# The three light experts of a streamed expert stage move from passes 2, 3 and 8 to passes 4, 6 and 8

## The chip, the cores and the metric

The kernel runs on one core of one Trainium2 chip. The metric is the device time of one execution in microseconds (us). Beside the runs that were only timed there is one profiled execution, and all rows below come from it.

## The reference, cut to what matters

An encoder trunk of two layers over 16 meta tokens and 256 frames, model width 1024. Each layer has a mixer (retention beside latent attention) and then a feed-forward part: a dense SwiGLU of width 3584 in the first layer, and eight SwiGLU experts of that width, of which each token takes two, in the second. A final RMS norm follows, and the meta tokens are dropped. The change touches only the order in which the expert part goes through its experts:

```python
def moe_swiglu(h, router_w, w_gate, w_up, w_down):
    logits = (h @ router_w).astype(jnp.float32)
    top_val, top_idx = lax.top_k(logits, TOP_K)
    gates = jax.nn.softmax(top_val, axis=-1)
    ...
    out = jnp.zeros_like(h)
    for e in range(N_EXPERTS):
        out = out + gate_dense[..., e:e + 1] * swiglu(h, w_gate[e], w_up[e], w_down[e])
    return out
```

## The kernel before, in words

Up to about 521 us the kernel runs the first layer, the mixer of the second, and the routing. Then come the experts, in eight **passes**. Everything is float32, and every expert's weights are streamed from HBM once: 24 **units** of 1792 KB, loaded two at a time as 12 **pairs** of 3584 KB (`load_two`, line 469, whose DMA is on line 473; single units, `load_one`, line 463, whose DMA is on line 466, at the very start and in the last half of the last expert).

**The ring.** The weights land in twelve slots, six pairs. SyncE (SP) issues the load of pair j only when TensorE has used up pair j - 6: it waits for `w_used` to reach `... + 2 * j + 2 - MOE_SLOTS` (line 471). TensorE adds to `w_used` as it finishes each unit. So the pair that TensorE works on and the five after it are all that can have landed or be on their way. All these loads go through one queue, in order.

**The passes.** For each expert, tokens are gathered into three tiles of 32 columns (capacity 96). For three **light** experts two tiles do (capacity 64), and TensorE leaves out tile 0: `tiles=LIGHT if it in LIGHT_AT` on line 1138, and `LIGHT` for the last pass on line 1143. A pass does `up` for four groups of columns (16 units) and then `down` (8 units). A light pass thus reads the same 44 MB of weights as a full one and does two thirds of the matmuls. The passes 0 to 5 are written out, the passes from 6 up to the last stand in a loop (line 1141), and the last one is always light. This text counts passes from 0 as the code does, so the last one is pass 7.

**Which expert stands where.** Expert 0 is always first, since its weights are loaded before the routing is known. The others are ranked by their number of tokens on VectorE (`ordering`, lines 1779 to 1808). The result, `at_pass`, gives each expert its pass: before, the lightest of the seven goes last (pass 7), the next two go to passes 1 and 2, and the rest follow by size. `order_sb` is the inverse table, which SP reads to know whose weights to load next (`ordered`, line 500); `order_ready` tells that it is there. GpSimd (POOL) uses `at_pass` to build the gather table (line 580).

**Around the passes.** ScalarE (ACT) applies the SiLU (L1385) and scales what leaves a pass (L1395), VectorE (DVE) multiplies and transposes (L1824, L1827), POOL gathers the tokens of a later pass (L625) and adds the results of the pass before into HBM (L634). ACT, DVE and POOL treat all passes alike, with three tiles. Each pass of ACT begins with the small copy on L1375.

Of the kernel before, what the change touches and what calls it, by code (L numbers as in the profile page):

```python
# [37 lines left out]
ALU = mybir.AluOpType  # L38
# [16 lines left out]
EXPERTS = 8  # L55
# [3 lines left out]
SMALL = CAP - TOK  # L59
LIGHT = range(TILES_OF - SMALL // TOK, TILES_OF)  # L60
LIGHTS = 3
LIGHT_AT = [EXPERTS - 1, *range(1, LIGHTS)]
BIG = 1e30
LATE_AT = 10240
GAIN_AT = 14000
# [114 lines left out]
def build(nc, stream, experts, h0, gains, router_w, fnorm, consts, out):  # L180
    with ExitStack() as ctx:
# [54 lines left out]
        at = [0]  # L236
# [112 lines left out]
        def col(c, n=P):  # L349
            return c_sb[:, c:c + n]  # L350
# [314 lines left out]
        def _(pe):  # L665
# [471 lines left out]
            for it in range(EXPERTS - 2):  # L1137
                expert(it, tiles=LIGHT if it in LIGHT_AT else range(TILES_OF), first=it == 0)
            pe.wait_ge(rounds_ready, 1)
# [319 lines left out]
        def _(dve):  # L1459
            V = nc.vector  # L1460
            chain = [0]

            def link(ins, inc=None):

                if inc is not None:
                    ins.then_inc(inc, 1)
                    dve.wait_ge(inc, 1)
                    return
                chain[0] += 1
                ins.then_inc(link_sem, 1)  # L1470
                dve.wait_ge(link_sem, chain[0])
# [266 lines left out]
            def routing():  # L1738
# [36 lines left out]
                link(V.reciprocal(v12[:, :, 3:4], v12[:, :, 3:4]))  # L1775
                V.tensor_tensor(v12[:, :, 2:3], v12[:, :, 2:3], v12[:, :, 3:4], ALU.mult).then_inc(gates_in, 1)
                ordering()

            def ordering():

                E = EXPERTS
                number, total = col(C_IOTA, E), bank[3][:, 0:E]
                size_rank, light, at = least[:, :], key[:, :], at_pass[:, :]
                by_size = cmp_a[:, 0:E, 0:E - 1]
                at_place = cmp_b[:, 0:E, :]
                dve.wait_ge(total_done, 1)
                link(V.scalar_tensor_tensor(out=key[:, :], in0=total, scalar=float(E), in1=number, op0=ALU.mult, op1=ALU.add))
                link(V.memset(key[:, 0:1], BIG))

                link(V.tensor_tensor(by_size, key[:, 1:E].unsqueeze(1).to_broadcast([P, E, E - 1]),  # L1790
                                     key[:, :].unsqueeze(2).to_broadcast([P, E, E - 1]), ALU.is_lt))
                link(V.tensor_reduce(size_rank, by_size, axis=AX.X, op=ALU.add))
                V.tensor_scalar(light, size_rank, float(LIGHTS), float(CAP - SMALL), ALU.is_lt, ALU.mult)
                link(V.tensor_scalar(at, size_rank, 0.0, E - 1.0, ALU.is_equal, ALU.mult))
                V.tensor_tensor(v_total, light, total, ALU.add)
                link(V.tensor_tensor(at, at, size_rank, ALU.add))
                link(V.memset(at[:, 0:1], 0.0))
                V.tensor_reduce(cnt[:, 0:1], v_total, axis=AX.X, op=ALU.max)
                link(V.tensor_tensor(at_place, at.unsqueeze(1).to_broadcast([P, E, E]),
                                     number.unsqueeze(2).to_broadcast([P, E, E]), ALU.is_equal))  # L1800
                V.tensor_scalar(cnt[:, 1:2], cnt[:, 0:1], float(CAP), float(PASSES - EXPERTS), ALU.is_gt, ALU.mult)
                V.tensor_scalar(cnt[:, 2:3], cnt[:, 0:1], float(CAP), float(ROUNDS - 1), ALU.is_gt, ALU.mult)
                link(V.tensor_tensor(at_place, at_place, number.unsqueeze(1).to_broadcast([P, E, E]), ALU.mult))
                V.tensor_scalar(rounds_sb[:, 1:2], cnt[:, 1:2], EXPERTS - 1.0, None, ALU.add)
                V.tensor_scalar(rounds_sb[:, 0:1], cnt[:, 2:3], 1.0, None, ALU.add).then_inc(rounds_ready, 1)
                link(V.tensor_reduce(v_total, at_place, axis=AX.X, op=ALU.add))
                V.scalar_tensor_tensor(out=at, in0=light, scalar=float(SLOT_COLS), in1=at, op0=ALU.mult, op1=ALU.add)
                link(V.tensor_copy(order_sb[:, :, 0], v_total), order_ready)
# [76 lines left out]
            for t in range(2):  # L1885
                if t:
# [7 lines left out]
                                       op0=ALU.mult, op1=ALU.mult).then_inc(res_ready, 1)  # L1894
# [115 lines left out]
```

## Time and profile before

| | us |
|---|---|
| median of 3 runs (lowest to highest) | 1352.09 (1351.71 to 1352.82) |
| profiled execution, its own time | 1352.45 |
| span of that execution, first to last instruction | 1350.6 |
| TensorE busy in the span | 1294.5 |
| expert passes, from about 521 us to the end of the last matmuls at about 1341 us | 820 |
| granted TensorE clock, mean | 0.988 |

The span is the part that the rows show; the profiled execution's own time has 1.85 us around it. Times in the trace are counted from the span's start. "PE" is TensorE's matmuls and "PEld" its weight loads, SPq is SyncE as it issues DMAs. A DMA's time to landing runs from its issue by SP until its semaphore tells that all of it is there, so it holds the time that it stood in the queue.

### The profile page before, as it was taken

The numbers are of one execution on the slowest core, as the hardware profiler recorded it, in microseconds if no ns is written. First come the engines' busy times: TensorE is split into PE (matmuls) and PEld (weight loads), VectorE is DVE, ScalarE is ACT, GpSimd is POOL, SyncE is SP. The second block draws the span as 40 slices with busy tenths as digits, with TensorE's granted clock in tenths as the row PEclk, the third lists the DMA queues.
The fourth block names the chain that finished last, engine by engine and source line by source line (L and its number), as shares of the span: only waits on it lengthen the run. The fifth ranks groups of instructions, "written<-read, shape, count | busy, mean of one in ns | idle before, by whom it ended". The sixth has DMA issues, their size and how long they took to land.

```text
span 1350.6 us, 31070 instructions
## 1 busy us (share of the span) xinstructions
PE 1294.5 (96%) x14058; PEld 887.0 (66%) x14058; DVE 469.0 (35%) x821; ACT 341.3 (25%) x593; POOL 83.4 (6%) x113
## 2 busy tenths in 40 slices
PE   9999999999999999999987889999999999999886
PEld 8889999999998996456452254465465456446333
DVE  7767866777687663110201000100100110110121
ACT  8666543334367643000100000000000000000011
POOL 0000000000000004201010001001001001001000
PEclk9999999999999999999999889999999999999999
DMA  9316555544442589999999999999999999999994
GB/s 371 112 63 242 200 183 187 188 165 179 170 150 72 185 321 424 417 417 412 422 429 419 432 427 419 432 428 416 431 427 421 429 427 426 421 429 425 414 425 189
DMA packets 34783, 443.89 MB, mean 329 GB/s; under 512 B 5664, under 2 KB 7840, under 8 KB 12256
## 3 DMA queue, kind: packets, MB, share of 16 engines
q1 hardware_dynamic: 28944, 434.14, 77.8%
q0 software_dynamic: 5424, 7.51, 2.0%
q8 instruction: 110, 1.80, 0.5%
q10 hardware_dynamic: 288, 0.29, 0.1%
q14 instruction: 17, 0.14, 0.0%
HBM read 438.20 MB, written 5.93 MB: 329 GB/s over the span
## 4 chain that ended last, share of the span: by engine, by line
PE 79%; DMA 16%; DVE 2%; ACT 2%; issue 1%; SPq 0%; ACTq 0%; DVEq 0%
PE bank L677 78%; DMA moe_pair<-experts 15%; DVE w_pairs L1476 1%; DMA ring<-stream 1%; PE bank L681 0%; PE bank L775 0%; DVE nmx L1561 0%; ACT scratch L1233 0%; PE bank L781 0%; ACT w_pairs L1155 0%; ACT scratch L1232 0%; ACT scratch L1230 0%; DVE parts L1490 0%; PE bank L1122 0%; DVE sq L1554 0%
## 5 line engine op out<-in xcount | busy, mean ns | idle before, releaser
L677 PE MATMUL bank<-moe_pair,hT 128*32 128x448 f32 x5376 | 517.1, 546 | 23.6 <-DMA moe_pair<-experts 22.8
L677 PE MATMUL bank<-parts,w_pairs 128*128 128x272 f32 (+1 forms) x3360 | 427.4, 289 | 1.5 <-DVE parts L1490 0.9
L677 PEld LDWEIGHTS bank<-parts,w_pairs 128*128 128x128 f32 x3360 | 421.8, 188 | 5.4 <-issue 2.7
L677 PEld LDWEIGHTS bank<-moe_pair,hT 128*32 128x32 f32 x5376 | 206.6, 111 | 330.1 <-issue 298.2
L1824 DVE SCALAR_TENSOR_TENSOR hT<-bank,slot_norm,scratch 128x224 f32<-128x224 f32 x96 | 40.6, 423 | 694.9 <-ACT scratch L1385 694.9
L677 PE MATMUL bank<-moe_pair,scratch 128*32 128x256 f32 x4704 | 263.5, 384 | 16.1 <-DMA moe_pair<-experts 16.1
L677 PEld LDWEIGHTS bank<-moe_pair,scratch 128*32 128x32 f32 x4704 | 184.3, 111 | 96.6 <-issue 25.0
L1476 DVE TENSOR_TENSOR w_pairs<-ring,w_pairs 128x2048 fp32r<-128x2048 f32 x68 | 154.7, 2290 | 32.2 <-ACT w_pairs L1155 32.1
L1385 ACT ACTIVATE scratch<-bank,norm_now 128x224 f32<-128x224 f32 x96 | 41.2, 446 | 492.3 <-PE bank L677 492.3
L1155 ACT ACTIVATE w_pairs<-ring 128x2048 fp32r<-128x2048 f32 x68 | 129.6, 1912 | 90.1 <-PE bank L677 90.0
L1395 ACT ACTIVATE scratch<-bank,slot_gate 128x256 f32<-128x256 f32 x21 | 9.2, 473 | 233.9 <-PE bank L677 233.9
L1708 DVE TENSOR_TENSOR hT<-hT,bank 128x272 f32<-128x272 f32 x112 | 48.7, 436 | 20.8 <-PE bank L677 19.8
L625 POOL DMA_INDIRECT scratch<-hn_rows,row_of x24 | 24.9, 1038 | 430.6 <-DVE hT L1841 424.8
L634 POOL DMA_INDIRECT acc_rows<-scratch,row_of x21 | 33.3, 1588 | 200.0 <-ACT scratch L1395 195.7
L1827 DVE STREAM_TRANSPOSE scratch<-hT 128x224 f32<-128x224 f32 x96 | 39.5, 411 | 3.3
L677 PE MATMUL bank<-scratch 128*128 128x256 f32 (+4 forms) x144 | 26.6, 353 | 1.3 <-ACT scratch L1248 1.3
L677 PEld LDWEIGHTS bank<-scratch 128*128 128x128 f32 (+1 forms) x144 | 21.8, 181 | 6.6 <-ACT scratch L1298 1.7
L1335 ACT ACTIVATE parts<-scratch 128x544 fp32r<-128x544 f32 x14 | 9.2, 659 | 58.8 <-DVE scratch L1723 58.8
L561 POOL TENSOR_TENSOR scratch<-scratch 128x16 f32<-128x16 f32 x4 | 0.9, 222 | 362.0 <-DVE scratch L1761 361.7
L1210 ACT ACTIVATE scratch<-bank 128x272 f32<-128x272 f32 (+2 forms) x52 | 19.7, 416 | 10.6 <-PE bank L677 9.9
L677 PE MATMUL bank<-scratch,ring 128*128 128x272 f32 (+1 forms) x64 | 15.3, 393 | 1.6 <-ACT scratch L1233 1.6
L677 PEld LDWEIGHTS bank<-scratch,ring 128*128 128x128 f32 x64 | 11.7, 190 | 4.6 <-ACT scratch L1233 2.7
(216 smaller groups left out, 487.6 us busy)
## 6 DMA issues: line engine op xcount, KB each, us to landing
moe_pair<-experts SPq DMA_DIRECT2D x84, 3584.0 KB, 38.6
ring<-stream SPq DMA_DIRECT2D x68, 1024.0 KB, 5.0
moe_pair<-experts SPq DMA_DIRECT2D x23, 1792.0 KB, 23.1
ring<-stream SPq DMA_DIRECT2D x4, 512.0 KB, 7.7
ring<-stream SPq DMA_DIRECT2D x2, 976.0 KB, 4.7
moe_pair<-experts SPq DMA_DIRECT2D x2, 896.0 KB, 44.5
ring<-stream SPq DMA_DIRECT2D x2, 768.0 KB, 10.3
hT<-h SPq DMA_DIRECT2D x4, 272.0 KB, 5.5
```

Source lines behind the costliest of these rows:

```text
L625: pool.indirect_dma_start(out=x_rows[:, s, :], out_offset=None, in_=hn_quarters, in_offset=bass.IndirectOffsetOnAxis(ap=row_of[:, s, n:n + ...
L634: pool.indirect_dma_start(out=acc_quarters, out_offset=bass.IndirectOffsetOnAxis(ap=row_of[:, s, n:n + 1], axis=0), in_=ye[:, s, :], in_of ...
L677: return release(nc.tensor.matmul(dst, lhsT, rhs, start=start, stop=stop), inc, count)
L1155: A(w_hi(n), slot(UNIT_OF[n]), ACT.Copy).then_inc(split_hi, 1)
L1210: A(dst[:, first_of(name, layer):], src(name, rows, cols), ACT.Copy).then_inc(out_free, 1)
L1335: A(ad_hi[c % 2], a_dense, ACT.Copy).then_inc(a_hi_ready, 1)
L1385: A(sil_moe[:, s, :], bank[UP_BANKS[g][s]][:, 0:FQ], ACT.Silu, scale=norm_now[:, s:s + 1]).then_inc(e_silu, 1)
L1395: A(ye[:, s, :], bank[DOWN_BANKS[s]][:, 0:256], ACT.Copy, scale=slot_gate[:, it, s:s + 1]).then_inc(ye_ready, 1)
L1476: V.tensor_tensor(w_lo(n), slot(UNIT_OF[n]), w_hi(n).bitcast(F32), ALU.subtract).then_inc(split_lo, 1)
L1708: V.tensor_tensor(hT[:, d, :], hT[:, d, :], bank[4 + d % 4][:, 0:L], ALU.add).then_inc(h_added, 1)
L1824: V.scalar_tensor_tensor(out=a_moe[:, s, :], in0=bank[UP_BANKS[g][s]][:, FQ:2 * FQ], scalar=slot_norm[:, it, s:s + 1], in1=sil_moe[:, s, : ...
L1827: V.transpose(ht[:, g, s, :], a_moe[:, s, :]).then_inc(ht_ready, 1)
```

## The change

`LIGHT_AT`, which tells TensorE which passes have two tiles, goes from passes 7, 1, 2 to passes 7, 5, 3. On VectorE the formula for an expert's pass follows. Before: rank 0 goes to 7, every other rank r to r, expert 0 (rank 7) to 0. After: ranks 0 to 3 go to 7 - 2r (7, 5, 3, 1) and ranks 4 to 7 to 14 - 2r (6, 4, 2, 0).

```diff
-LIGHT_AT = [EXPERTS - 1, *range(1, LIGHTS)]
+LIGHT_AT = [EXPERTS - 1 - 2 * r for r in range(LIGHTS)]
...
                 V.tensor_scalar(light, size_rank, float(LIGHTS), float(CAP - SMALL), ALU.is_lt, ALU.mult)
-                link(V.tensor_scalar(at, size_rank, 0.0, E - 1.0, ALU.is_equal, ALU.mult))
+                link(V.tensor_scalar(at, size_rank, float(E // 2), float(E - 1), ALU.is_ge, ALU.mult))
+                link(V.scalar_tensor_tensor(out=at, in0=size_rank, scalar=-2.0, in1=at, op0=ALU.mult, op1=ALU.add))
                 V.tensor_tensor(v_total, light, total, ALU.add)
-                link(V.tensor_tensor(at, at, size_rank, ALU.add))
-                link(V.memset(at[:, 0:1], 0.0))
+                link(V.tensor_scalar(at, at, E - 1.0, None, ALU.add))
                 V.tensor_reduce(cnt[:, 0:1], v_total, axis=AX.X, op=ALU.max)
```

The kinds of passes, in order: before F L L F F F F L, after F F F L F L F L (F full, L light).

## Rows read from the trace of the kernel before

**Rows 1.** The page: span, busy time, GB/s of 40 slices, the weight loads.
```profile
span 1350.6 us, 31070 instructions
PE 1294.5 (96%) x14058; PEld 887.0 (66%) x14058; DVE 469.0 (35%) x821; ACT 341.3 (25%) x593; POOL 83.4 (6%) x113
...
GB/s 371 112 63 242 200 183 187 188 165 179 170 150 72 185 321 424 417 417 412 422 429 419 432 427 419 432 428 416 431 427 421 429 427 426 421 429 425 414 425 189
...
moe_pair<-experts SPq DMA_DIRECT2D x84, 3584.0 KB, 38.6
moe_pair<-experts SPq DMA_DIRECT2D x23, 1792.0 KB, 23.1
```

**Rows 2.** The chain of waits in order of time: start, us, what.
```profile
521.52 150.76 PE bank L677 x1888
...
672.44 34.42 DMA moe_pair<-experts
...
812.26 433.92 PE bank L677 x5760
...
1289.31 43.12 DMA moe_pair<-experts
```

**Rows 3.** Stretches about as long as passes 0, 1, 2, 3 and 6, then the last.
```profile
core 0: us, PE busy (x) PEld busy (x) DVE busy (x) ACT busy (x) POOL busy (x), PEclk, DMA share, GB/s
521.50:629.40 107.90, 107.88 (x1432) 56.46 (x1436) 12.93 (x47) 7.00 (x15) 19.81 (x42) 1.00 1.00 418
629.40:704.00 74.60, 72.90 (x976) 37.82 (x968) 10.39 (x27) 6.36 (x17) 7.92 (x6) 1.00 1.01 422
704.00:812.00 108.00, 85.00 (x968) 36.08 (x960) 10.39 (x27) 7.17 (x20) 7.88 (x6) 0.91 1.01 427
812.00:920.20 108.20, 107.94 (x1432) 56.42 (x1436) 10.38 (x27) 5.78 (x16) 7.86 (x6) 1.00 1.01 426
1137.00:1245.40 108.40, 108.40 (x1448) 55.75 (x1443) 10.38 (x27) 6.90 (x17) 7.86 (x6) 1.00 1.01 425
1245.40:1332.40 87.00, 73.18 (x864) 30.55 (x856) 13.21 (x31) 7.81 (x19) 6.15 (x5) 0.96 0.95 398
```

**Rows 4.** L473 issued in 1137 to 1238 (pass 6), then in 630 to 697 (pass 1).
```profile
L473 SPq DMA_DIRECT2D moe_pair<-experts x12: 332/333/341, 1137.9 to 1237.3; - x12
...
L473 SPq DMA_DIRECT2D moe_pair<-experts x12: 332/333/342, 630.3 to 696.6; - x12
```

**Rows 5.** L473 issued in 678 to 1247; landing of its first and its last.
```profile
L473 SPq DMA_DIRECT2D moe_pair<-experts x65: 332/333/341, 678.5 to 1246.3; - x65
...
DMA to landing us min/median/max: 37.0/37.0/37.0
...
DMA to landing us min/median/max: 35.0/35.0/35.0
```

**Rows 6.** L473 issued in 545 to 636; landing of the one at 630.3.
```profile
L473 SPq DMA_DIRECT2D moe_pair<-experts x10: 328/332/353, 548.8 to 630.3; - x10
...
DMA to landing us min/median/max: 13.0/13.9/14.5
...
DMA to landing us min/median/max: 14.2/14.2/14.2
```

**Rows 7.** Two stretches by window (columns as in rows 3).
```profile
580.00:640.00 60.00, 60.00 (x928) 36.45 (x924) 3.33 (x9) 2.91 (x8) 7.82 (x6) 1.00 1.00 415
670.00:680.00 10.00, 10.00 (x125) 4.75 (x121) 1.81 (x5) 1.20 (x3) 0.00 (x0) 1.00 1.00 433
```

**Rows 8.** The L473 issued at 811.5: issue and landing.
```profile
L473 SPq DMA_DIRECT2D moe_pair<-experts x1: 333/333/333, 811.5 to 811.5; - x1
DMA to landing us min/median/max: 45.0/45.0/45.0
```

**Rows 9.** The first three L466 (469 to 482) and their landing.
```profile
L466 SPq DMA_DIRECT2D moe_pair<-experts x3: 328/328/637, 469.8 to 481.0; - x3
DMA to landing us min/median/max: 6.9/7.0/10.9
```

**Rows 10.** VectorE's operations of the ordering.
```profile
L1796 DVE TENSOR_TENSOR at_pass<-at_pass,least x1: 159/159/159, 522.8 to 522.8; 128x8 f32<-128x8 f32 x1
...
L1797 DVE MEMSET at_pass<- x1: 59/59/59, 523.0 to 523.0; 128x1 f32 x1
...
L1807 DVE SCALAR_TENSOR_TENSOR at_pass<-key,at_pass 128x8 f32<-128x8 f32 x1 | 0.2, 167 | 0.0
```

## The prediction, made before the changed kernel ran

> **What bounds the kernel now.** I read the page first [rows 1]: TensorE is busy 96% of the span, which invites the thought that any idle time taken from it is time won. But from slice 15 on the transfers run at 412 to 432 GB/s in every slice but the last. The chain of waits [rows 2] shows both: 150.8 us of matmuls, then transfers, then 433.9 us of matmuls, then transfers to the end. Stretch by stretch [rows 3] passes 0, 3 and 6 are bound by TensorE (busy 108.4 of 108.4 us), pass 2 and the last pass wait for weights (busy 85.0 of 108.0 and 73.2 of 87.0), and yet the DMA share stays at 1.00 or more from 521 to 1245 us. Two clocks tick side by side, so I price both.
>
> TensorE's pace: in a full pass SP issues a pair whenever TensorE has used one, 12 issues from 1137.9 to 1237.3 [rows 4], so 99.4/11 = 9.04 us for a pair, 108.4 for a pass. In a light pass, 66.3/11 = 6.03 us and 72.3 for a pass [rows 4].
>
> The transfers' pace with a deep queue: the 65 pairs issued from 678.5 to 1246.3 landed from 678.5 + 37.0 = 715.5 to 1246.3 + 35.0 = 1281.3 [rows 5]; 565.8/64 = 8.84 us for a pair, 106.1 for a pass. That holds the gathers and the additions into HBM. Where these are absent it is faster: 433 GB/s [rows 7], 8.5 us for 3.67 MB.
>
> So a full pass is 2.3 us slower than its weights, a light one 33.8 us faster. Eight passes of weights need 8 x 106.1 = 849; of TensorE, 5 x 108.4 + 3 x 72.3 = 759. **The transfers are the total bound**, and a wait of TensorE costs nothing as long as the queue never runs dry. What can cost is a queue that runs dry: the ring holds six pairs, and where TensorE lags, SP must wait before it issues more.
>
> How full the queue is shows in the time to landing. At 678.5, 811.5 and 1246.3 us it is 37.0, 45.0 and 35.0 [rows 5, 8], four or five pairs deep. In pass 0 it is 13.0 to 14.5 [rows 6], one pair and a half. That is nearly dry: in 580 to 640, after the routing's own traffic, 415 GB/s was moved [rows 7], against 422 to 427 over passes 1 to 6 [rows 3], and the landings follow TensorE's 9.04 us, not 8.84. The light pass 1 ends this: it frees a pair every 6.03 us and fills the queue, which stays deep until the end. In passes 3 to 6 the queue loses only 0.2 us a pair.
>
> **The change, part by part.**
>
> *The ordering on VectorE* [rows 10]. One tensor_scalar stays, a tensor_tensor (159 ns) and a memset (59 ns) go, a scalar_tensor_tensor (167 ns) and a tensor_scalar of its size (I take 159) come: +0.1 us, with as many linked steps as before. Behind it stand the gather table on POOL and pass 0's second group on TensorE, and what POOL gathers with it is for pass 1, 100 us later; TensorE does not need the order before its group 1. Cost 0; if the cover were gone, 0.1 us.
>
> *The work moved.* Bytes, matmuls, gathers and DMA issues are as many as before: eight passes, three light. SP's loop has the same waits, and POOL's gathers and additions are tied to passes, in the same order. All that moves is when TensorE frees pairs.
>
> *Passes 1 and 2 become full.* After pass 0, SP issued a pair at 630.3 [rows 6], and its landing took 14.2 us. With 24 more pairs at 9.04, SP issues the pair that is 24 further on at 630.3 + 217.0 = 847.3. Before, the same pair was issued at 811.5 and landed 45.0 later, at 856.5 [rows 8]. So all depends on how long it takes from a late issue to landing with a shallow queue. With 13.0 to 14.2 as in pass 0 it lands at 860.3 to 861.5, **3.8 to 5.0 us later than before**. The rates say the same: 24 x (9.04 - 8.84) = 4.8 if the queue has no depth left to give. And the bandwidth: 217 us at 415 instead of 425 GB/s lose 5.1. I take 4.8.
>
> The bounds of this term. From below: a shallow queue might give back more depth. The nearest row is the single unit of 1792 KB, which landed in 6.9 us [rows 9]; its bytes at 433 GB/s take 4.2, so 2.7 go to all else. A pair alone would take 8.5 + 2.7 = 11.2, landing at 858.5, a loss of 2.0. That the loss is 0 would need 9.2 us, less than this row allows. From above: the additions into HBM of pass 2's results come after 847 now and not at 812. A pass has 106.1 - 12 x 8.5 = 4 us of other traffic, gathers and additions; half of it, 2 us, may now have to be paid after the late landing and not before: 5.0 + 2 = 7. I stay near pass 0's own rows, since it is the same state, ring and pace.
>
> The Trainium skill (DMA: Bandwidth & Descriptors, Anatomy of one DMA) puts the fixed cost of a DMA at about 2.0 us on top of its bytes, in a fit for the GpSimd path. By that a lone pair would land in 10.5 us, the loss would be 1.3 us and the time 1353.4. It speaks against my term; pass 0's 13.0 at best doesn't agree with it, and I give the page's figure no more than a part of the first rival's chance.
>
> *Pass 3 becomes light.* TensorE begins it at about 846, with the transfers ahead by 5 x 9.04 - 14.2 = 31 us. In the pass it gains 12 x (8.84 - 6.03) = 33.7, so it runs free to its last pair and waits some 2 us there. From here the queue is deep again and the transfers don't rest. *Pass 4* (full) runs at TensorE's pace, ending near 1032. *Pass 5* (light) now takes the wait that stood in pass 2: it ends when its weights have come, near 1133. *Pass 6* ends near 1243 (before 1245.4), and the *last pass* has its weights 4.8 us later than before. It begins almost without a lead, so it waits for nearly every pair; before it had some 10 us of lead to use up. That costs nothing, as the end is the last landing.
>
> **Sum:** 1352.45 + 4.8 = 1357.25 for the profiled execution. That execution stood 0.36 us above the median of the runs, so I forecast a median of 1356.9.
>
> **The rivals.**
>
> *The queue gives back depth, and the loss is too small to see* (22%). If the time to landing goes down to 11.2 in passes 1 and 2, the loss is 2.0 us and the time 1354.1; if these passes have less other traffic than pass 0 and the transfers don't rest, as the DMA share of 1.00 in pass 0 could be read, it is 1352.1. For: pass 0 had 13.0 once, and its traffic from the gather table is gone later. Against: 415 GB/s, after that traffic. A measurement of this kernel tells about 0.2% (2.7 us) from no change, so this is the case "same".
>
> *TensorE's waits are spread better, and it is faster* (6%). Passes 1 and 2 had most of TensorE's waiting, 23 us in pass 2 [rows 3]. If the deep queue were not what limits the end but TensorE's late finish of pass 6 were, then the end would go with that: pass 5's last weights at 1122 without a loss, pass 6 over by about 1238, 7 us sooner, and 1345. It decides from the point where the last pass is bound by TensorE. Against it: in the last pass TensorE waits already, 73.2 busy of 87.0 [rows 3].
>
> *A second loss at the end* (7%). TensorE waits longer in pass 5 and the last, and the granted clock is 0.91 where it waits in pass 2 and 0.96 in the last pass [rows 3], so some stretches run at 1.2 and not at 2.4 GHz. The full pass 6 follows such a stretch, and the last matmuls and the tail may fall into one. The last pass lost (1 - 0.96) x 87 = 3.5 us of clock; if as much stood where nothing hides it, 4.8 + 3.5 = 8.3, 1360.4. Against: with transfers as the bound, a slow stretch of TensorE in mid-pass is hidden, and only the last 1 or 2 us of matmuls lie behind the last landing.
>
> *The change does nothing* (in the 22%): LIGHT_AT and the ordering could disagree. By the formula ranks 0, 1, 2 stand at 7, 5, 3, where TensorE has two tiles, so they don't.
>
> **How the numbers follow.** The forecast, a loss of 2.7 to 7 us, has 65%. Slower by over 0.2%: 65 + 7 = 72%. Within 0.2%: 22%. Faster: 6%. The range of 8 in 10 goes from 1353.4, which takes in the bound of 2.0 us, to 1360.0, which takes in the bound of 7; it leaves out the cases of no loss, the faster one and most of the second loss.
>
> **What would show it.** In the changed profile: the pairs issued in 630 to 847 us take 11 to 15 us to landing, where before they took 14 rising to 46; GB/s in that stretch near 415; TensorE without a wait from 521 to about 918; an issue at 847.3; the landing of that pair at about 861. Then times to landing that climb to 40 and more in pass 3, TensorE's waits in pass 5 and in the last, and a last landing about 5 us later. I am wrong if GB/s in 630 to 847 is 423 or more, if the pair of 847.3 lands before 858.5, or if the last landing is late and the end isn't.

## The result, and the profile after

| | before | changed |
|---|---|---|
| median, us (runs) | 1352.46 (7) | 1356.74 (7) |
| lowest to highest | 1351.71 to 1353.75 | 1355.18 to 1357.34 |
| ratio, 95% interval | | 1.0028 [1.0019, 1.0037] |
| span of the profiled execution | 1350.6 | 1354.9 |

The medians differ by 4.3 us; the ratio makes it 3.8 us, with an interval of 2.6 to 5.0. The forecast was 1356.9.

The page of the changed kernel: span, busy time, and GB/s in 40 slices, which answer to [rows 1].

```profile
span 1354.9 us, 31070 instructions
PE 1295.4 (96%) x14058; PEld 878.2 (65%) x14058; DVE 468.8 (35%) x821; ACT 341.2 (25%) x593; POOL 85.4 (6%) x113
...
GB/s 370 111 63 248 200 175 187 187 180 164 184 134 91 186 324 425 418 418 405 427 404 412 421 409 416 409 428 422 427 430 423 426 427 426 425 427 427 416 425 208
```

TensorE's busy time is the same within a microsecond. What differs is slices 18 to 25 of GB/s (610 to 881 us, slices counted from 0): 404 to 421 but for one of 427, where in [rows 1] there stands 412 to 432.

The chain of waits of the changed kernel (start, us, what):

```profile
521.25 367.59 PE bank L677 x4768
...
889.01 34.38 DMA moe_pair<-experts
...
923.53 116.37 PE bank L677 x1504
...
1089.50 45.03 DMA moe_pair<-experts
1134.54 0.04 issue
1134.58 110.37 PE bank L677 x1440
...
1293.04 43.69 DMA moe_pair<-experts
```

Against [rows 2] the first stretch of matmuls has grown from 150.8 to 367.6 us, and it is the one that matters. In it TensorE sets when slots come free, and with them when transfers may start.

Busy time by stretch, passes 0, 1 with 2, then 3, 4, 5, 6 and the last; the columns are those of [rows 3].

```profile
521.50:629.40 107.90, 107.90 (x1436) 56.38 (x1432) 12.80 (x45) 6.97 (x16) 19.64 (x42) 1.00 1.00 420
630.00:847.00 217.00, 217.00 (x2888) 113.52 (x2884) 20.77 (x54) 14.00 (x36) 15.81 (x12) 1.00 1.00 412
847.00:922.00 75.00, 72.21 (x960) 37.14 (x951) 10.38 (x27) 6.33 (x18) 7.86 (x6) 1.00 1.01 421
922.00:1034.00 112.00, 110.47 (x1444) 57.36 (x1448) 10.38 (x27) 6.62 (x17) 7.88 (x6) 0.98 1.01 426
1034.00:1133.00 99.00, 80.97 (x960) 36.36 (x952) 10.38 (x27) 6.34 (x19) 7.86 (x6) 0.93 1.01 426
1133.00:1245.50 112.50, 110.92 (x1452) 47.56 (x1456) 10.38 (x27) 7.17 (x19) 7.90 (x7) 0.98 1.01 426
1245.50:1336.70 91.20, 72.52 (x844) 28.55 (x836) 13.20 (x31) 6.51 (x17) 6.11 (x5) 0.96 0.98 408
```

And the same window of the kernel before:

```profile
630.00:847.00 217.00, 192.03 (x2296) 88.11 (x2292) 23.13 (x60) 14.69 (x41) 20.55 (x15) 0.95 1.01 424
```

In 217 us the changed kernel moved 412 GB/s instead of 424 while TensorE was busy all the time, not 192 us of it. TensorE looks better, and the kernel is slower: 12 x 217 / 425 is 6 us of transfers. That is a rough estimate, above the 4.6 us that the pair below shows: a rate is rounded to 1 GB/s, which is 0.5 us here, and the window before holds nine of POOL's additions where the one after holds six. The DMA share hardly tells the two apart, with 1.01 and 1.00. A rate in GB/s and the times to landing show the loss.

Cut finer, GB/s shows where it lies. Forty slices of 640 to 847 us, first before, then changed:

```profile
GB/s 388 435 389 440 422 424 438 430 432 413 438 438 424 421 424 424 394 425 415 438 432 441 432 416 430 438 438 419 425 439 410 441 443 424 410 426 414 412 410 426
```

```profile
GB/s 359 439 423 416 438 430 427 347 438 391 438 427 380 430 414 414 424 419 427 391 381 389 434 418 427 424 421 435 360 424 427 421 424 321 438 415 432 419 419 430
```

Before, no slice of 5.2 us is under 388. After, six are, down to 321; the others lie at 389 to 439.

Of the changed kernel, the DMA issues of L473 in 630 to 847 us, then those in 921 to 1246, each with the time to landing:

```profile
L473 SPq DMA_DIRECT2D moe_pair<-experts x25: 332/333/342, 630.1 to 846.9; - x25
...
DMA to landing us min/median/max: 13.2/14.1/15.2
...
L473 SPq DMA_DIRECT2D moe_pair<-experts x37: 332/333/341, 921.5 to 1245.1; - x37
...
DMA to landing us min/median/max: 39.8/41.5/46.7
```

For 25 issues in a row the queue holds some 14 us of work and not more. The last of them, at 846.9, took 14.2 us and landed at 861.1; the same pair landed at 856.5 before [rows 8].

```profile
L473 SPq DMA_DIRECT2D moe_pair<-experts x1: 333/333/333, 846.9 to 846.9; - x1
...
DMA to landing us min/median/max: 14.2/14.2/14.2
```

The last unit of all comes in two halves. First those of the kernel before, then those of the changed one:

```profile
L466 SPq DMA_DIRECT2D moe_pair<-experts x2: 2474/3480/4485, 1289.8 to 1292.5; - x2
...
DMA to landing us min/median/max: 44.3/44.5/44.8
```

```profile
L466 SPq DMA_DIRECT2D moe_pair<-experts x2: 2205/3260/4314, 1293.6 to 1296.0; - x2
...
DMA to landing us min/median/max: 45.1/45.2/45.3
```

The very last transfer landed at 1341.1 (issued at 1296.0, 45.1 us) where it was 1336.8 (1292.5 and 44.3): 4.3 later. From there to the end of the span both take 13.8 us.

### The profile page after: what moved, and what is told of

Same layout as the page of the kernel before. It is cut to its first block, busy times and chain, and to the rows that moved or that the text cites. A ratio compares the mean times of both kernels' runs of the same rounds, so it can differ in the third digit from the quotient of the medians.

```text
span 1354.9 us, 31070 instructions
## 1 busy us (share of the span) xinstructions
PE 1295.4 (96%) x14058; PEld 878.2 (65%) x14058; DVE 468.8 (35%) x821; ACT 341.2 (25%) x593; POOL 85.4 (6%) x113
## 4 chain that ended last, share of the span: by engine, by line
PE 79%; DMA 16%; DVE 3%; ACT 2%; issue 1%; SPq 0%; ACTq 0%; DVEq 0%
PE bank L677 77%; DMA moe_pair<-experts 15%; DVE w_pairs L1476 1%; DMA ring<-stream 1%; PE bank L681 0%; PE bank L775 0%; DVE nmx L1561 0%; ACT scratch L1233 0%; PE bank L781 0%; ACT w_pairs L1155 0%; ACT scratch L1232 0%; ACT sq L1175 0%; ACT scratch L1230 0%; DVE parts L1490 0%; PE bank L1122 0%
## 5 line engine op out<-in xcount | busy, mean ns | idle before, releaser
L677 PEld LDWEIGHTS bank<-moe_pair,hT 128*32 128x32 f32 x5376 | 201.3, 111 | 338.7 <-issue 304.4
L677 PEld LDWEIGHTS bank<-moe_pair,scratch 128*32 128x32 f32 x4704 | 180.4, 111 | 101.9 <-issue 20.3
## 6 DMA issues: line engine op xcount, KB each, us to landing
ring<-stream SPq DMA_DIRECT2D x2, 768.0 KB, 10.5
```

Source lines behind the costliest of these rows:

```text
L677: return release(nc.tensor.matmul(dst, lhsT, rhs, start=start, stop=stop), inc, count)
```

## The experiments

The theory, in short: while the queue is shallow, a pair lands when TensorE frees a slot plus some 14 us, so a full pass takes TensorE's 108.4 us and not the transfers' 106.1. Once a light pass has filled the queue, the transfers never rest. The rival: the loss comes from the late half, where TensorE waits in pass 5 and the last pass, at a lower granted clock, and has no lead when the last pass begins.

### Where the first light pass stands (e1 to e4)

The kernel before, with the three light passes elsewhere. The pass of each rank is written out, which adds 12 small linked operations to VectorE's ordering and takes 2 away; the rest of the kernel is untouched. For e1:

```diff
-LIGHT_AT = [EXPERTS - 1, *range(1, LIGHTS)]
+LIGHT_AT = [EXPERTS - 1, 1, 5]
+PLACE = [7, 1, 5, 2, 3, 4, 6, 0]
...
+                for r in range(1, E - 1):
+                    link(V.tensor_scalar(v_total, size_rank, float(r), float(PLACE[r]), ALU.is_equal, ALU.mult))
+                    link(V.tensor_tensor(at, at, v_total, ALU.add))
-                link(V.tensor_tensor(at, at, size_rank, ALU.add))
-                link(V.memset(at[:, 0:1], 0.0))
```

e2, e3 and e4 have 2 and 3, 3 and 4, 4 and 5 in place of 1 and 5.

Expected of e1:

> Light passes 1, 5 and 7. It shares its last four passes (F L F L) with the changed kernel and its first three (F L F) with the kernel before. Theory (the transfers rest in full passes that follow pass 0 while only about 14 us of work stand in the queue; about 2.2 us for each such pass, and nothing once a light pass has filled the queue): the same time as the kernel before, 1352 to 1353 us; times to landing above 30 us from pass 2 on; the last landing near 1337. Rival (the loss comes from the late half: TensorE waits more in pass 5 and in the last pass, at a lower granted clock, and starts the last pass with no lead): slower by 3 to 4.3 us, like the changed kernel.

Expected of e2:

> Light passes 2, 3 and 7: one full pass (1) between pass 0 and the first light one. Theory: half of the changed kernel's loss, +2.2 us (1.5 to 3), 1354.6. The pair that SP issued at 846.9 in the changed kernel is freed by TensorE at about 811 here. Rival (late half): no loss, since pass 6 and the last pass look as they do in the kernel before.

Expected of e3:

> Light passes 3, 4 and 7: as many full passes before the first light one as in the changed kernel (0, 1, 2), but the lights together and the full passes 5 and 6 before the last. Theory: the same loss as the changed kernel, +4.3 us (3.5 to 5), 1356.7. Rival (late half, the spacing of the light passes): less than half of it, since TensorE has a lead again at the start of the last pass: 0 to +2.

Expected of e4:

> Light passes 4, 5 and 7: three full passes after pass 0. Theory: +6.5 us (5.5 to 7.5), 1359; times to landing of 13 to 15 us up to about 955 us, where TensorE ends pass 3. Rival (late half): the loss of the changed kernel at most, +4.3. A third outcome, that the queue's loss ends once the routing's traffic is past, would give no more than +4.3 either.

| kernel | light passes | full passes between pass 0 and the first light one | median | over before (1352.42) | ratio, 95% | last landing |
|---|---|---|---|---|---|---|
| before | 1, 2, 7 | 0 | 1352.42 | | | 1336.8 |
| e1 | 1, 5, 7 | 0 | 1353.22 | 0.8 | 1.0005 [0.9996, 1.0014] | 1337.0 |
| e2 | 2, 3, 7 | 1 | 1355.06 | 2.6 | 1.0020 [1.0011, 1.0029] | 1339.2 |
| e3 | 3, 4, 7 | 2 | 1356.78 | 4.4 | 1.0031 [1.0019, 1.0043] | 1340.8 |
| changed | 3, 5, 7 | 2 | 1356.74 | 4.3, in its own comparison | 1.0028 [1.0019, 1.0037] | 1341.1 |
| e4 | 4, 5, 7 | 3 | 1359.48 | 7.1 | 1.0052 [1.0039, 1.0066] | 1343.8 |

The loss goes by one number, the full passes between pass 0 and the first light one, at 2.0 to 2.6 us each. e1 shares its last four passes with the changed kernel and loses nothing that can be told, and e3, with its lights together, loses as much as the changed kernel. The rival had both the other way round. e4 still loses in its third full pass, so the loss does not end with the routing's traffic either. The stretch of short times to landing grows with it. e4, issues in 630 to 948 us (the line is L474 there):

```profile
L474 SPq DMA_DIRECT2D moe_pair<-experts x36: 332/333/342, 630.6 to 946.8; - x36
DMA to landing us min/median/max: 12.8/14.2/15.5
```

and e1, from 690 to 1245 us, where the queue stays deep:

```profile
L474 SPq DMA_DIRECT2D moe_pair<-experts x63: 332/333/342, 690.7 to 1239.4; - x63
DMA to landing us min/median/max: 37.1/42.1/46.6
```

### More on the way from the same ring: single units (e5, e6)

```diff
-                sp.wait_ge(w_used, it * EXPERT_UNITS + (MOE_SPLIT + 2 * j + 2 - MOE_SLOTS))
-                p = 2 * j % MOE_SLOTS
-                sp.dma_start(moe_pairs[MOE_PLACES[p] // 2][:, :], experts[e * (EXPERT_UNITS // 2) + j]).then_inc(moe_in[p], 16)
+                for m in (2 * j, 2 * j + 1):
+                    sp.wait_ge(w_used, it * EXPERT_UNITS + (MOE_SPLIT + m + 1 - MOE_SLOTS))
+                    load_one(e[m % 2] if isinstance(e, list) else e, m)
```

TensorE waits for each unit then, and SP reads the expert's number twice. e5 is the changed kernel, e6 the kernel before.

> The changed kernel, but SP frees and loads the ring by single units (1792 KB) in all passes, not by pairs: half a pair more of the ring can be on its way. Theory (too little in the queue in passes 0 to 2): the queue has up to 4.5 us more of work in it, more than the 4.8 us that passes 1 and 2 take from it less what it can give, so the loss against the same edit of the kernel before (e6) goes from 4.3 to under 1.5 us. Smaller DMAs may move less per us, so the two times themselves may lie above or below 1352; only their difference tells. Rival (late half, or anything that is tied to the order of the passes): the difference stays at 3 to 4.5 us.

> The kernel before with the same single units. Theory: if smaller DMAs are as fast, 0 to 2 us faster than the kernel before, since pass 0 is short of queued work too; if they are 0.5% slower, about 4 us slower. The difference of e5 to this run: under 1.5 us by the theory, 3 to 4.5 by the rival.

e5 took 1358.73 us, 1.0045 [1.0031, 1.0058] of before; e6 1358.34, 1.0044 [1.0030, 1.0058]. The loss between the two orders went from 4.3 to 0.4 us in the medians, and to 1.4 in the last landings (1343.7 and 1342.3). The five runs of e5 lie within 3.3 us of each other and those of e6 within 1.6, so the difference is known to some 2 us only; it is below 4.3. e5's issues (L466) at 631.2, and then in 835 to 849 us:

```profile
L466 SPq DMA_DIRECT2D moe_pair<-experts x1: 333/333/333, 631.2 to 631.2; - x1
DMA to landing us min/median/max: 14.4/14.4/14.4
...
L466 SPq DMA_DIRECT2D moe_pair<-experts x4: 332/333/333, 835.1 to 848.1; - x4
DMA to landing us min/median/max: 10.9/11.5/12.2
```

With units the time to landing goes from 14.4 down to 10.9 to 12.2 over passes 1 and 2: the queue gives back 2 to 3 us where the pairs gave back none. That is the first rival of the prediction at work, in another kernel. It is not all of the difference. In e6, where the queue is deep, the transfers are slower too: the units issued at 630.2 and 812.6 landed at 644.2 and 858.1, 24 pairs apart, so two units take 8.91 us against 8.83 for the same pairs before (644.5 to 856.5). Against TensorE's 9.04 two full passes then have only 24 x 0.13 = 3 us to lose. It is no remedy: both orders are 0.4% slower than with pairs, which is more than the order is worth.

### Less other traffic (e7 to e10)

The additions of each pass's result into HBM are taken out. First each was replaced by a DMA of 64 bytes, to keep the semaphores (e7 the changed kernel, e8 the one before):

```diff
-                    pool.indirect_dma_start(
-                        out=acc_quarters, ... compute_op=ALU.add).then_inc(acc_out, 16)
+                    pool.dma_start(acc_rows[TILES_OF * n + s:TILES_OF * n + s + 1, 0:16], ye[0:1, s, 0:16]).then_inc(acc_out, 16)
```

> The changed kernel without the additions of the passes' results into HBM: each is replaced by a DMA of 64 bytes, so the results of passes 0 to 6 are left out of the output. Theory: in passes 1 and 2 the transfers go at TensorE's pace whatever else they have to do, and where the queue is deep they gain some 1.8 us a pass. So both kernels get faster, this one by less: 1345 to 1348, against e8 a loss of 6 to 8 us instead of 4.3. Rival (the loss comes from bursts of other traffic that meet a shallow queue): the loss shrinks, to under 3 us.

> The kernel before with the same additions left out. Theory: 10 to 13 us faster than the kernel before (seven bursts of about 1.8 us, less the one in pass 0), 1339 to 1342.

Both expectations failed, and the edit with them: e7 took 1358.07 (1.0040 [1.0026, 1.0053]) and e8 1353.70 (1.0001 [0.9992, 1.0010]), no faster than with the additions; the loss between them stayed at 4.4. The stretch after pass 1, 704 to 716 us, first of the kernel before, then of e8:

```profile
704.00:716.00 12.00, 8.80 (x80) 3.18 (x76) 0.00 (x0) 1.39 (x5) 4.76 (x3) 0.86 1.00 427
```

```profile
704.00:716.00 12.00, 8.71 (x76) 3.26 (x80) 0.00 (x0) 0.63 (x4) 1.55 (x3) 0.86 0.99 374
```

With three DMAs of 64 bytes the rate is 374 GB/s and not 427 for these 12 us, 1.5 us of transfers. So this pair of runs took nothing away and says nothing on the theory. e9 (the changed kernel) and e10 (the one before) leave the additions out with nothing in their place, and drop what waited for them:

```diff
-                    pool.indirect_dma_start(
-                        out=acc_quarters, ... compute_op=ALU.add).then_inc(acc_out, 16)
...
-                act.wait_ge(acc_out, it * (16 * TILES_OF) + 16)
+                act.wait_ge(acc_out, 16)
...
-                pool.wait_ge(acc_out, 16 + 16 * TILES_OF * (count - 1))
+                pool.wait_ge(acc_out, 16)
```

> The changed kernel with the additions of the passes' results into HBM left out altogether, with no small DMA in their place (e7 and e8 had one of 64 bytes, and it cost the stream as much as the additions), so the results of passes 0 to 6 are missing from the output. Theory: the issue at 846.9 stays where it is, since TensorE sets it, and only the deep part after it gains: 1345 to 1348; the time to landing may go down to 11.2 to 13 us before the light pass. Against e10 a loss of 6 to 8 us. Rival (bursts of other traffic on a shallow queue are what costs): a loss under 3 us.

> The kernel before with the same additions left out. Theory: the queue is deep from pass 1 on, so nearly every addition's traffic comes off the time: 1339 to 1342.

e9: 1350.45 us, 0.9981 [0.9972, 0.9990] of before (1352.81 in this comparison). e10: 1342.97, 0.9923 [0.9909, 0.9936]. Both gain less than I expected (1345 to 1348 and 1339 to 1342); the last landing of e10 is 8.4 us earlier than before (1328.4), 1.2 us for each of seven bursts and not 1.8. That of e9 (1335.7) is 5.4 us earlier than the changed kernel's, so some 3 us less: about the two bursts that fall into its shallow stretch. But the loss between the orders grew from 4.3 to 7.5 us, as the theory had it (6 to 8) and the rival of bursts did not (under 3). e9 in the window of passes 1 and 2:

```profile
630.00:847.00 217.00, 217.00 (x2888) 113.54 (x2884) 20.76 (x54) 14.00 (x35) 6.05 (x6) 1.00 0.99 411
```

That is 411 GB/s against the changed kernel's 412, with two bursts fewer to carry: TensorE sets the pace there, and work that is taken from the transfers buys nothing. Its issue at 847.2 took 14.9 us to landing; 11.2 to 13 was expected as possible and did not come.

### A light pass 0, and a smaller ring (e11, e12)

e11 is the changed kernel with two tiles in pass 0; tile 0 of expert 0 isn't computed:

```diff
-                expert(it, tiles=LIGHT if it in LIGHT_AT else range(TILES_OF), first=it == 0)
+                expert(it, tiles=LIGHT if it == 0 or it in LIGHT_AT else range(TILES_OF), first=it == 0)
```

> The changed kernel with two tiles in pass 0 too; tile 0 of expert 0, 32 of its 96 columns, is left out of the computation. Theory: pass 0 then fills the queue (to about 45 us), passes 1 and 2 take about 5 us from it and the transfers never rest: the loss is gone, 1350 to 1352.5, at or a little below the kernel before, though all passes from 1 on are those of the changed kernel. Rival (late half, or the order as such): 1355 to 1357, for the end is bound by the transfers and TensorE's time in pass 0 can't matter to it.

It took 1352.29 us, 0.9991 [0.9982, 1.0000] of before, and its last landing, at 1336.9, is that of the kernel before: the loss is gone, though passes 1 to 7 are those of the changed kernel. Pass 0 is 36 us shorter here, so the full passes 1 and 2 stand in 594 to 810 us. Their windows, and the issues in 594 to 1245:

```profile
594.00:702.00 108.00, 105.65 (x1392) 54.23 (x1388) 10.38 (x27) 6.76 (x17) 7.93 (x6) 1.00 1.01 425
702.00:810.00 108.00, 108.00 (x1440) 56.40 (x1436) 10.39 (x27) 6.91 (x17) 7.88 (x6) 1.00 1.01 426
```

```profile
L473 SPq DMA_DIRECT2D moe_pair<-experts x73: 332/333/341, 598.9 to 1239.9; - x73
DMA to landing us min/median/max: 38.1/42.2/47.8
```

The same full passes at 425 and 426 GB/s instead of 412. What they cost is set by the queue that they find.

e12 is the changed kernel with a ring of five pairs:

```diff
-                sp.wait_ge(w_used, it * EXPERT_UNITS + (MOE_SPLIT + 2 * j + 2 - MOE_SLOTS))
+                sp.wait_ge(w_used, it * EXPERT_UNITS + (MOE_SPLIT + 2 * j + 4 - MOE_SLOTS))
```

> The changed kernel with one pair less of the ring in use: SP issues a pair when TensorE has used up pair j - 5. Theory: where the queue is shallow, landing is TensorE's freeing of a slot plus 13 to 15 us, so all of passes 0 to 2 lands one pair of TensorE's pace (9.04 us) later, the pair of 846.9 is issued at 855.9, and the end moves by as much: +9 us on the changed kernel, 1365 to 1367. Where the queue is deep a pair less of it costs nothing. Rival (the ring's depth is no limit and the loss is in the late half): within 2 us of the changed kernel.

It took 1364.77 us, 1.0088 [1.0074, 1.0102] of before, so 8.0 more than the changed kernel's median in its own comparison; the last landing, at 1349.1, is also 8.0 later. Its issues in 545 to 847 us:

```profile
L473 SPq DMA_DIRECT2D moe_pair<-experts x34: 327/333/353, 548.3 to 846.6; - x34
DMA to landing us min/median/max: 12.6/13.4/14.3
```

One pair less, and the shallow stretch is as shallow as before, a pair's time later. It is a steady state: each pair lands 12.6 to 14.3 us after TensorE frees its slot here, and 13.2 to 15.2 with the ring of six pairs. The 9.04 us expected came out as 8.0, and the expectation had a step wrong: the pair that the changed kernel issues at 846.9 was to be issued at 855.9. But the slot that it now waits for is freed in the light pass 3, 6.0 us later and not 9.0:

```profile
L473 SPq DMA_DIRECT2D moe_pair<-experts x1: 332/332/332, 852.6 to 852.6; - x1
...
DMA to landing us min/median/max: 17.0/17.0/17.0
```

It lands at 869.6, behind the pair before it, 8.5 us later than in the changed kernel: about one pair at the transfers' pace.

## Why the prediction was right

**The bound.** The transfers bound the total, and the way to lose time was to let them rest. The forecast named the place (passes 1 and 2), the marker (time to landing of 11 to 15 us) and the pair to watch. SP was to issue it at 847.3 and it was to land at 860.3 to 861.5; the trace has 846.9 and 861.1. The term of 4.8 us measured 4.6 at that pair, 4.3 at the last landing and 4.3 in the medians. That the forecast of 1356.9 lies within 0.2 us of 1356.74 is in part luck: it stood on the median of three runs, 1352.09, which is 0.4 us below that of all seven, and its term is 0.5 us above 4.3. The two errors cancel. One figure of its working can mislead: the 849 us for all eight passes of weights is more than the 820 us of the passes, because the loading begins at 469.8 us [rows 9], before pass 0.

**The bounds of the term.** The lower one, 2.0 us, took a lone pair's 11.2 us. No pair of any run here landed in less than 12.6, so it was not reached. Only single units, which have half the bytes, came below. The Trainium skill (DMA: Bandwidth & Descriptors, Anatomy of one DMA) gives a fixed cost of about 2.0 us per DMA, fitted for DMAs that GpSimd issues, which the prediction turned into an estimate of 10.5 us for a lone pair. The paced pairs of this stretch took 13.2 to 15.2; no run here has a pair by itself, so the figure is not tested. The upper one, 7, charged 2 us for additions that now come after the late landing. They cost nothing more that can be seen: from the landing of the watched pair to the last landing it is 480.0 us after (861.1 to 1341.1) and 480.3 before (856.5 to 1336.8).

**The rest of the passes.** The ordering on VectorE was put at nothing, and the issue that passes 0 to 2 lead to came 0.4 us before its forecast. TensorE's wait at the end of pass 3 was put at 2 us and the trace has 2.1. Passes 4, 5 and 6 were to end at 1032, 1133 and 1243; ScalarE's small copy, which begins a pass there, stands at 1034.5, 1133.3 and 1245.5. The granted clock is 0.98 in passes 4 and 6, which the forecast left out for them. Passes 4 and 6 take about 112 us and not 108.4, with a wait of 2.2 us for weights in each. It costs nothing in the end, as the prediction said of a slow stretch that the transfers hide.

**The rivals.** The queue gave back nothing with pairs: 14.2 us at 630.1, and 14.2 at 846.9 (e5 shows that it can with units). TensorE's waits were spread, but not fewer where it counts: it is busy 72.5 of 91.2 us in the last stretch, 73.2 of 87.0 before [rows 3], so the case of a faster kernel had no footing. A second loss at the end did not come: 13.8 us from the last landing to the end, both times. e1 has these late waits too and no loss.

**What stays open.** Why a pair takes 13 to 15 us in the steady state, where bytes alone take 8.5 and the estimate for a lone pair was 11.2, isn't shown. Single units reach 10.9, but they have half the bytes and are issued twice as often, and which of the two does it isn't shown. A pair by itself was not measured.

## What to carry to other kernels

In a ring that streams weights, the queue's depth is a stock: a pass that computes faster than its weights arrive fills it, one that computes slower empties it, and once it is at its floor every further slow pass costs the whole difference of the two paces (here 108.4 - 106.1 us). So put a fast pass as early as possible, and don't spread the fast ones to even out the compute engine's waits: here those waits stood where the queue was deep. This holds where the transfers bound the total, as here. Read the time to landing of the DMAs and GB/s, not TensorE's busy share nor the DMA share: in the slower kernel's stretch of loss the first looked better, and the second fell only from 1.01 to 1.00.

## What the runs showed of the hardware

Three DMAs of 64 bytes from GpSimd's queue cost the running stream about as much as three additions of rows into HBM. The rate was 374 GB/s over 12 us where it was 427 with the additions, whose own bytes count in it. By the last landings a burst costs 1.4 us in e8 (1338.4 against e10's 1328.4, seven bursts) and 1.2 us with the additions. Why so few bytes cost that much isn't shown.

Loads of 1792 KB, rows of 14336 bytes, made the whole kernel 0.44% slower (interval 0.30 to 0.58%) than loads of 3584 KB with rows of 28672 (e6 against before), with as many bytes and a deep queue. Whether the size of a DMA, the length of its rows or the number of issues does it wasn't separated.
